# Layer 0's mixer: gate and value columns first, convolution taps spread between later columns, sample taps on GpSimd, weight loads in the queue of the cache copies

## The chip, the cores and the metric

The kernel runs on one core of a Trainium2 chip. The metric is the device time in microseconds (us) of one execution. Before the change three runs gave a median of 2352.38 us (2351.0 to 2361.53).

## What is computed

Two layers of a decoder trunk are evaluated for a prompt of 256 tokens and for 8 samples of 4 tokens each (288 tokens in all, model width 1024, everything in fp32). Only layer 0's mixer is touched. Cut to what matters:

```
z = h @ w_in                                   # 3072 columns and 8 gate columns
glu = z[..., :D_A] * sigmoid(z[..., D_A:o1])   # A: 512 value and 512 gate columns
ca, new_buf_a = causal_dwconv(glu, buf_a, conv_a_w)          # 31 taps per channel
ya = silu(layernorm(ca + conv_a_b, ln_a_g, ln_a_b))
qkv, new_buf_qkv = causal_dwconv(z[..., o1:o2], buf_qkv, conv_qkv_w)   # 1536 columns, 4 taps
q, k = l2norm(silu(q)), l2norm(silu(k))
od, s_new = gated_delta(q, k, v, g, beta, s0)  # chunks of 64 tokens, a triangular solve in each
od = rmsnorm(od, gdn_norm_g) * silu(gate)      # 512 "out" columns
mixed = concat([ya, od]) @ w_out
```

The program must also return the caches of layer 1: for each sample all cached rows but the oldest are copied from an input in HBM to an output in HBM. Those copies depend on nothing and are issued from the start of layer 0's mixer on.

## The kernel before

Channels lie on the 128 partitions and tokens along the free axis. The projection is made in 24 **columns** of 128 channels. A column is 8 accumulating matmuls of 128x128 weights against the 288 tokens, and goes into bank 6 or 7 of PSUM in turn (`acc_of`); so column j may only start when column j-2 has been read out. Weights come in six loads of 2 MB, each holding four columns, into the two slots of `wring` (slot 0 for even loads, slot 1 for odd ones); loads 0 and 1 are issued before the mixer begins.

Each engine runs its own program, and semaphores join them. `col_ready` counts columns that TensorE has finished; `z_ready`, `sig_done`, `glu_done` and `gate_done` count columns that were read out.

The first part of the mixer is written out by hand. It makes the 12 q/k/v columns. ScalarE copies each to SBUF (`take`), VectorE runs its four taps (`convolve`), ScalarE applies silu and squares (`silu`), and TensorE adds up the squares (`sums`). At its end the roots are spread over the partitions (`widen`), q and k are normalized, and the last rows of q/k/v are turned and stored (`q_tails`, `copy_tail`, counted by `tail_q_out`).

The second part is made of lanes: `tile(0)` and `tile(1)` (128 prompt tokens each) and `tile(2)` (the 32 sample tokens) build and solve the triangular systems; `branch()` does all of A, and `main()` walks the four chunks and finishes. Each lane yields a number, its key, ahead of each step, and the step with the smallest key goes next. This fixes the order in which each engine's instructions are written. Steps of a tile have keys 0, 1, 2, ...; `main` starts at 40. In `branch()` the 12 columns of A (4 gate, 4 value, 4 out) start at key 5.5, and the 4 x 31 taps, each an instruction on the prompt and one on the samples, are spread from key 9 up to the layer norm of A at key 50.5.

SyncE issues the small loads, then the 43 cache copies (`roll(n)` issues the next n) in groups of 4, 16 and 23. Before the last group it waits for `tail_q_out`. Then it issues the stores of the new states; it waits for `main`'s last chunk before `out_delta_p`, and its last instruction in the mixer waits until all 14 of its stores have landed (`stored`):

```
sp.wait_ge(turn[2], len(order[2]))
for b in range(DEC_B):
    sp.dma_start(T["out_delta_s"][0, b].rearrange("h k v -> k h v"), S0[:, b, :, :]
                 ).then_inc(stored, 16)
sp.wait_ge(stored, 16 * (6 + DEC_B))
```

The block ends when all engines have come to its end, and layer 0's tail (the expert lookup, which gathers rows of a table in HBM) begins only then. ScalarE issues loads 2 to 5 of the columns' weights and the two of the output projection, in a queue of its own.

Of the kernel before, what the change touches and what calls it, by code (L numbers as in the profile page):

```python
# [16 lines left out]
ALU = mybir.AluOpType  # L17
# [3 lines left out]
D = 1024  # L21
KC = D // 128
# [200 lines left out]
QC = [4, 5, 6, 7, 0, 1, 2, 3, 8, 9, 10, 11]  # L223


def conv_delta_phase(nc, K, T, wring, w_in, w_out_in, mixT, rolls):
# [18 lines left out]
    job_key = lambda j, half: 5.5 + 1.15 * (2 * j + half)  # L245
    JOBS_A = [(kind, c) for c in range(4) for kind in ("gate", "value")] + [("out", c) for c in range(4)]
    MEAN_KEY = MAIN + 10.5
# [16 lines left out]
    with ExitStack() as ctx:  # L264
# [29 lines left out]
        dec, decT = per_tile("decay", [128, 4, 128]), per_tile("decayT", [128, 4, 128])  # L294
# [3 lines left out]
        inT = P.sb("intraT", [128, 3, 4, 128])  # L298
# [18 lines left out]
        a_ready, sig_done, glu_done, gate_done, ca_ready, ln_ready, ln_root, ya_ready, ya_done = (  # L317
            P.sem(n) for n in ("a_ready", "sig_done", "glu_done", "gate_done", "ca_ready", "ln_ready",
# [30 lines left out]
        with nc.Block() as block:  # L349
            @block.sync  # L350
            def _(sp):
# [41 lines left out]
            def _(pe):  # L393
                mm = nc.tensor.matmul

                def column(i):
                    s = i // 4
                    if i % 4 == 0:
                        pe.wait_ge(w_in[s % 2], 16 * (s // 2 + 1))
                    if i >= 2:  # L400
                        pe.wait_ge(z_ready, i - 1)
                    for k in range(KC):
                        last = mm(acc_of(i), wring[:, s % 2, k, i % 4 * 128:i % 4 * 128 + 128], hT[:, k, :],
                                  start=(k == 0), stop=(k == KC - 1))
# [28 lines left out]
                def tile(t):  # L433
# [66 lines left out]
                    for hd in range(GH):  # L500
                        mm(cols_of(t, 0)[:, hd, :], vs[:, hd, :], inT[0:NS, 2, hd, 0:NS], start=True, stop=True)
# [12 lines left out]
                def branch():  # L514

                    for j, (kind, c) in enumerate(JOBS_A):
                        s = {"gate": 3, "value": 4, "out": 5}[kind]
                        for half in range(2):
                            yield job_key(j, half)
                            if half == 0:  # L520
                                pe.wait_ge(w_in[s % 2], 16 * (s // 2 + 1))
                                if j == 0:
                                    pe.wait_ge(z_ready, 11)
# [1986 lines left out]
```

## Time and profile before

| | |
|---|---|
| median of 3 runs | 2352.38 us |
| profiled execution, its own time | 2358.02 us |
| its span | 2356.2 us |
| layer 0's mixer in it | 21.0 to 323.0 us |
| busy share of the span: TensorE / VectorE / ScalarE / GpSimd | 84% / 55% / 32% / 28% |
| mean rate of all transfers | 371 GB/s |

Times in rows are microseconds from the start of the span. In a timeline row the first number is the start, the second the length; "x16" says how many instructions were merged. An engine's name with a q (SPq) is its queue of DMA issues: such a row says when transfers were handed over, not when they landed. A matmul in fp32 appears as two rows' worth of instructions, so a column is x16. "PEclk" is the granted clock of TensorE as a share of 2.4 GHz.

### The profile page before, as it was taken

How to read it: one execution, taken by the hardware profiler on the slowest of the kernel's cores; microseconds unless marked ns; L12 is line 12 of the kernel's file. 1: busy time of each engine (PE TensorE's matmuls, PEld its weight loads, DVE VectorE, ACT ScalarE, POOL GpSimd, SP SyncE). 2: the span in 40 equal slices, each digit the busy share in tenths (PEclk: the TensorE clock that was granted, in tenths of full speed). 3: DMA queues.
4: the chain of work that ended last, by engine and by line, in shares of the span. 5: the costliest groups of instructions: out<-in, count | busy, mean ns of one | idle time of the engine just before them, and what ended most of it. 6: DMA issues, size and time to landing. Idle time of an engine off the chain costs nothing. (4 is left out here: it accounts for less than half of the span.)

```text
span 2356.2 us, 25516 instructions
## 1 busy us (share of the span) xinstructions
PE 1977.2 (84%) x8902; PEld 966.3 (41%) x8902; DVE 1298.6 (55%) x3308; ACT 757.8 (32%) x2225; POOL 653.9 (28%) x650
## 2 busy tenths in 40 slices
PE   7799779887788888866999999989887788888765
PEld 5578645442233332222435654555443233332221
DVE  4485948666667766654100311038666667766754
ACT  3200014343334434433111221124343344434443
POOL 0000004443344354331010000104443444444441
PEclk9897789998999999977999999999999999999977
DMA  9999959999999999997997787828999999999995
GB/s 316 370 333 352 363 194 362 427 426 428 427 427 427 423 405 427 427 427 283 384 392 266 275 308 303 311 112 337 427 427 427 426 427 427 426 427 427 427 427 228
DMA packets 123903, 874.97 MB, mean 371 GB/s; under 512 B 19742, under 2 KB 29726, under 8 KB 38775
## 3 DMA queue, kind: packets, MB, share of 16 engines
q0 software_dynamic: 92160, 662.74, 67.5%
q1 hardware_dynamic: 30751, 198.03, 23.0%
q10 hardware_dynamic: 864, 12.58, 1.4%
q8 instruction: 70, 1.15, 0.2%
q14 instruction: 58, 0.48, 0.1%
HBM read 861.99 MB, written 118.81 MB: 416 GB/s over the span
## 5 line engine op out<-in xcount | busy, mean ns | idle before, releaser
L1570 PE MATMUL tail_acc<-tail_ring,tail_diag 128*128 128x512 f32 x1248 | 617.5, 623 | 131.8 <-ACT tail_diag L1417 130.7
L1717 POOL DMA_INDIRECT tail_ring<-in_peer_uv,tail_idx x348 | 364.9, 1049 | 862.3 <-PE tail_acc L1570 452.6
L1296 DVE CUSTOM_DVE_ANT_0 tail_ring<-tail_ring,all_h 128x1024 f32<-128x1024 f32 x348 | 424.2, 1223 | 261.2 <-DMA tail_ring<-in_peer_uv,tail_idx 259.1
L1570 PE MATMUL tail_acc<-mid_wring,tail_diag 128*128 128x512 f32 x800 | 391.7, 621 | 70.9 <-ACT tail_diag L1417 70.7
L1570 PEld LDWEIGHTS tail_acc<-tail_ring,tail_diag 128*128 128x128 f32 x1248 | 221.4, 193 | 504.0 <-ACT tail_diag L1417 323.2
L1296 DVE CUSTOM_DVE_ANT_0 mid_wring<-mid_wring,all_h 128x1024 f32<-128x1024 f32 x228 | 278.6, 1224 | 172.3 <-DMA mid_wring<-in_peer_uv,tail_idx 172.0
L1409 ACT ACTIVATE tail_gelus<-tail_dots 128x1 f32<-128x1 f32 x576 | 116.4, 202 | 722.5 <-DVE tail_dots L1296 722.1
L1717 POOL DMA_INDIRECT mid_wring<-in_peer_uv,tail_idx x228 | 251.0, 1101 | 319.6 <-PE tail_acc L1570 267.1
L1838 PE MATMUL mix_acc<-mid_wring,all_hT 128*128 128x512 f32 x576 | 273.8, 611 | 1.5 <-PEq L80 1.4
L1570 PEld LDWEIGHTS tail_acc<-mid_wring,tail_diag 128*128 128x128 f32 x800 | 143.8, 194 | 301.8 <-ACT tail_diag L1417 181.5
L1417 ACT ACTIVATE tail_diag<-all_ident,tail_weights 128x128 f32<-128x128 f32 x512 | 205.5, 401 | 24.3 <-PE tail_acc L1570 7.8
L1414 ACT ACTIVATE tail_weights<-tail_gelus,tail_gate 128x1 f32<-128x1 f32 x576 | 169.8, 295 | 18.7
L1838 PEld LDWEIGHTS mix_acc<-mid_wring,all_hT 128*128 128x128 f32 x576 | 103.4, 194 | 110.9 <-issue 110.3
L2062 DVE TENSOR_TENSOR mix_r<-mix_acc,mix_rope 128x128 f32<-128x128 f32 x24 | 7.0, 292 | 188.5 <-ACT mix_rows L2172 188.5
L2089 DVE SCALAR_TENSOR_TENSOR mix_s<-mix_scores_p,mix_band 128x384 f32<-128x384 f32 (+1 forms) x12 | 9.1, 755 | 124.5 <-PE mix_scores_p L1953 124.4
L2379 POOL DMA_DIRECT2D mix_ring<-in_kT x32 | 17.0, 532 | 213.5 <-PE mix_wide L1879 177.7
L1530 PEld LDWEIGHTS tail_spare<-all_hT,tail_w_big 128*128 128x128 f32 x512 | 67.0, 191 | 14.9 <-issue 14.6
L1530 PE MATMUL tail_spare<-all_hT,tail_w_big 128*128 128x128 f32 (+1 forms) x512 | 68.6, 288 | 2.1 <-ACT all_hT L1382 2.1
L1493 PE MATMUL tail_acc<-mid_wring,all_mixT 128*128 128x512 f32 x128 | 60.9, 635 | 3.9 <-PEq L80 3.9
L533 PE MATMUL mix_banks<-all_hT,mid_wring 128*128 128x288 f32 x192 | 56.5, 452 | 3.5 <-DMA mid_wring<-in_w_ab 3.5
L2379 POOL DMA_DIRECT2D mix_ring<-in_v_rows x32 | 16.9, 528 | 149.0 <-PE mix_wide L1916 130.6
L868 DVE SCALAR_TENSOR_TENSOR all_mixT<-mix_padded_a,mix_taps_a,all_mixT 128x256 f32<-128x256 f32 x120 | 56.6, 472 | 0.8
(399 smaller groups left out, 2017.0 us busy)
## 6 DMA issues: line engine op xcount, KB each, us to landing
mid_wring<-in_w_qkv SPq DMA_DIRECT2D x18, 2048.0 KB, 8.9
mix_ring<-in_kT POOLq DMA_DIRECT2D x16, 1024.0 KB, 9.6
mix_ring<-in_v_rows POOLq DMA_DIRECT2D x16, 1024.0 KB, 9.7
out_kv_s<-in_cache_kv_w SPq DMA_DIRECT2D x8, 2016.0 KB, 69.1
mix_ring<-in_kT POOLq DMA_DIRECT2D x16, 768.0 KB, 11.2
mix_ring<-in_v_rows POOLq DMA_DIRECT2D x16, 768.0 KB, 8.6
mid_wring<-in_w_ab ACTq DMA_DIRECT2D x4, 2048.0 KB, 27.2
tail_w_big<-in_w_query SPq DMA_DIRECT2D x8, 1024.0 KB, 11.3
```

Of the source, the lines that this page charges most:

```text
L533: last = mm(acc_of(j), wring[:, s % 2, k, c * 128:c * 128 + 128], hT[:, k, :], start=(k == 0), stop=(k == KC - 1))
L868: ch.step(STT(out=ca[:, c, 0:SEQ], in0=pa[:, c, k:k + SEQ], scalar=wa[:, c, k:k + 1], in1=ca[:, c, 0:SEQ], op0=ALU.mult, op1=ALU.add))
L1296: V.tensor_tensor_reduce(out=u, in0=u, in1=h[:, g, :], scale=1.0, scalar=0.0, op0=ALU.mult, op1=ALU.add, accum_out=dots[:, n:n + 1]).then_ ...
L1409: ch(A(gelus[:, n:n + 1], dots[:, n:n + 1], ACT.Gelu))
L1414: ch(A(weights[:, n:n + 1], gelus[:, n:n + 1], ACT.Copy, scale=gate[:, j, i:i + 1]))
L1417: A(diag[:, n % DIAGS, 0:w], idn[:, 0:w], ACT.Copy, scale=weights[:, n:n + 1]).then_inc(diag_ready, 1)
L1493: last = mm(acc[g][:, c * 512:(c + 1) * 512], mixT[:, k, g * 128:g * 128 + 128], wring[:, c, k, :], start=(k == 0), stop=(k == KC - 1))
L1530: last = mm(sp2[:, i % 2 * 512:i % 2 * 512 + hi - lo], w_query[:, n, k, :], hT[:, k, lo:hi], start=(k == 0), stop=(k == KC - 1))
L1570: last = mm(acc[g][:, c * 512:(c + 1) * 512], diag[:, n % DIAGS, :], v[:, c * 512:(c + 1) * 512], start=first, stop=final)
L1717: pool.indirect_dma_start(slot(r), None, table, bass.IndirectOffsetOnAxis(ap=idx[:, j, i:i + 1], axis=0)).then_inc(landed[r], 16)
L1838: last = mm(acc_of(n), hT[:, kc, o:o + p], w[:, kc, :], start=(kc == 0), stop=(kc == KC - 1))
L2379: pool.dma_start(ring[:, sl % SLOTS_AHEAD, 0:hi - lo], T[name][half, b, :, lo:hi]).then_inc(landed[sl % SLOTS_AHEAD], 16)
```

## The change

The columns come in another order: gate 0, value 0, ..., gate 3, value 3, then the 12 of q/k/v, then the 4 "out" ones. All have one function `column(j)`. Two out columns stand in the written-out part and two in the lanes, at keys 7.5 and 10.5. The taps of A on the prompt are handed out one by one by `tap(n)`: in runs between the gated columns, one after each of the four steps of `convolve` and one at its end, and the last 15 at the start of the lanes. A tap waits for the previous tap of its own channel group only. The taps on the samples leave VectorE: GpSimd multiplies windows of 31 by the taps and adds them up in a tree. `sums` of a q/k column stands three columns later on TensorE. The layer norm of A moves from key 50.5 to 20.5. `decay`, `decayT` and `intraT` of the sample tile become 32 wide. All weight loads move from ScalarE's queue into SyncE's, and the copies are issued between them.

```diff
+AB_COLUMNS = [4, 0, 5, 1, 6, 2, 7, 3] + [8 + n for n in QC] + [20, 21, 22, 23]
-    job_key = lambda j, half: 5.5 + 1.15 * (2 * j + half)
-    MEAN_KEY = MAIN + 10.5
+    OUT_KEYS = {22: 7.5, 23: 10.5}
+    TAILS_KEY = 13.5
+    MEAN_KEY = 20.5
...
-                roll(4)
-                sp.dma_start(S0[:].rearrange("p b h n -> p (b h n)"), T["state_rows"]).then_inc(state_in, 16)
+                for s in range(2, 6):
+                    sp.wait_ge(col_ready, 4 * (s - 1))
+                    sp.dma_start(wring[:, s % 2], T["w_ab"][:, s]).then_inc(w_in[s % 2], 16)
+                    if s == 2:
+                        sp.dma_start(S0[:].rearrange("p b h n -> p (b h n)"), T["state_rows"]).then_inc(state_in, 16)
+                        roll(2)
+                    else:
+                        roll(3)
                 sp.dma_start(T["out_conv_a_s"][0, :, 0:26, :], T["state_conv_a"][0, :, 4:30, :]).then_inc(stored, 16)
-                roll(16)
+                for half in range(2):
+                    sp.wait_ge(col_ready, 20 + 4 * half)
+                    sp.dma_start(wring[:, half], T["w_out0"][:, half]).then_inc(w_out_in[half], 16)
+                    roll(2)
                 sp.wait_ge(tail_q_out, 3)
...
+                for j in range(8, 11):
+                    column(j)
+                for j in range(11, 20):
+                    column(j)
+                    if j < 19:
+                        sums(j - 11)
+                column(20)
                 q_tails(0)
                 q_tails(1)
                 for i in range(8):
                     widen(i)
                 q_tails(2)
+                column(21)
                 lanes.run()
...
-                def load(s):
-                    nc.scalar.dma_start(wring[:, s % 2], T["w_ab"][:, s]).then_inc(w_in[s % 2], 16)
...
+                pool.wait_ge(a_in, 32)
+                for c in range(4):
...
+                    pool.wait_ge(glu_done, c + 1)
+                    ch(G.tensor_tensor(windows[:], shifted, taps_of, ALU.mult))
+                    terms = windows[:].rearrange("p b t k -> p (b t) k")
+                    ch(G.tensor_tensor(terms[:, :, 0:15], terms[:, :, 0:15], terms[:, :, 16:31], ALU.add))
+                    for n in (8, 4, 2):
+                        ch(G.tensor_tensor(terms[:, :, 0:n], terms[:, :, 0:n], terms[:, :, n:2 * n], ALU.add))
+                    ch(G.tensor_tensor(dst, terms[:, :, 0], terms[:, :, 1], ALU.add))
+                    G.tensor_scalar(dst, dst, wa[:, c, 31:32], None, ALU.add).then_inc(samples_done, 1)
...
+                begin_at = (0, 19, 31, 36)
+                taps = sorted(((c, k) for c in range(4) for k in range(CAW)), key=lambda e: (begin_at[e[0]] + e[1], e[0]))
```

**SyncE's queue in the mixer before.** After the small loads come 4 copies (`out_kv_s<-in_cache_kv_w`; 16x15872 is 1.02 MB, 32x16384 is 2.10 MB), the sample states and the other copies:

```order
L371 DMA mix_sample_a<-in_hist_a 128x32x30
L358 DMA out_kv_s<-in_cache_kv_w 16x15872 x4
L374 DMA mix_S_sample<-in_state_rows 128x4096
L375 DMA out_conv_a_s<-in_state_conv_a 8x13312
L358 DMA out_kv_s<-in_cache_kv_w 16x15872 x4
```

After these stand 12 more copies, the two stores behind `tail_q_out`, the other 23 copies, and the stores of the end:

```order
L379 DMA out_conv_qkv_s<-all_h 24x1536
L358 DMA out_kv_s<-in_cache_kv_w 32x16384
L358 DMA out_kv_s<-in_cache_kv_w 32x16128
L358 DMA out_kv_s<-in_cache_kv_w 32x16384
L358 DMA out_kv_s<-in_cache_kv_w 32x16128
L358 DMA out_kv_s<-in_cache_kv_w 32x16384 x19
L382 DMA out_conv_a_p<-all_h 30x512
```

**The same queue of the change.** L382 and L391 are the weight loads, each behind a wait for columns (for 4, 8, 12 and 16 at L382, for 20 and 24 at L391):

```order
L378 DMA mix_sample_a<-in_hist_a 128x32x30
L382 DMA mid_wring<-in_w_ab 128x4096
L384 DMA mix_S_sample<-in_state_rows 128x4096
L365 DMA out_kv_s<-in_cache_kv_w 16x15872 x2
L382 DMA mid_wring<-in_w_ab 128x4096
L365 DMA out_kv_s<-in_cache_kv_w 16x15872 x3
L382 DMA mid_wring<-in_w_ab 128x4096
L365 DMA out_kv_s<-in_cache_kv_w 16x15872 x3
L382 DMA mid_wring<-in_w_ab 128x4096
```

```order
L391 DMA mid_wring<-in_w_out 128x4096
L365 DMA out_kv_s<-in_cache_kv_w 32x16128
L365 DMA out_kv_s<-in_cache_kv_w 32x16384
L391 DMA mid_wring<-in_w_out 128x4096
L365 DMA out_kv_s<-in_cache_kv_w 32x16128
L365 DMA out_kv_s<-in_cache_kv_w 32x16384
L394 DMA out_conv_qkv_p<-all_h 3x1536
```

Between them stand 3 copies of 2 MB and the first `out_conv_a_s`. So 13 copies stand ahead of the second L391 and 30 behind it; the stores of the end (`out_delta_p`, `out_delta_s` x8) stand behind all of them, as before.

**VectorE in a q/k/v column before**, where prompt and sample steps (L753, L756) alternate:

```order
L750 TENSOR_SCALAR mix_conv<-mix_padded_q,mix_taps_q 128x256
L751 TENSOR_SCALAR mix_conv<-mix_sample_q,mix_taps_q 128x32
L753 SCALAR_TENSOR_TENSOR mix_conv<-mix_padded_q,mix_taps_q,mix_conv 128x256
L756 SCALAR_TENSOR_TENSOR mix_conv<-mix_sample_q,mix_taps_q,mix_conv 128x32
L753 SCALAR_TENSOR_TENSOR mix_conv<-mix_padded_q,mix_taps_q,mix_conv 128x256
```

**And of the change**, with a tap of A (L759, into `all_mixT`) behind each pair:

```order
L784 TENSOR_SCALAR mix_conv<-mix_sample_q,mix_taps_q 128x32
L759 SCALAR_TENSOR_TENSOR all_mixT<-mix_padded_a,mix_taps_a,all_mixT 128x256
L788 SCALAR_TENSOR_TENSOR mix_conv<-mix_padded_q,mix_taps_q,mix_conv 128x256
L792 SCALAR_TENSOR_TENSOR mix_conv<-mix_sample_q,mix_taps_q,mix_conv 128x32
L759 SCALAR_TENSOR_TENSOR all_mixT<-mix_padded_a,mix_taps_a,all_mixT 128x256
```

Five taps of A go with each q/k/v column.

**TensorE at the first level of the solve, before** (L461 is the last step of "rows", L467 the step "P 0" of the tiles, L533 columns of A, whole ones at x8 and a half at x4):

```order
L461 MATMUL mix_banks<-all_ident,mix_conv 32x128
L533 MATMUL mix_banks<-all_hT,mid_wring 128x288 x8
L467 MATMUL mix_banks<-mix_decayT,mix_g_wide 128x128 x8
L467 MATMUL mix_banks<-mix_decayT,mix_g_wide 32x32 x4
L533 MATMUL mix_banks<-all_hT,mid_wring 128x288 x4
L473 MATMUL mix_banks<-mix_decay,mix_padded_q 128x128
```

**And of the change**, where the first L420 is column 22 and the second column 23, the last of all 24 (L478 is "rows", L484 is "P 0"):

```order
L478 MATMUL mix_banks<-all_ident,mix_conv 32x128
L420 MATMUL mix_banks<-all_hT,mid_wring 128x288 x8
L484 MATMUL mix_banks<-mix_decayT,mix_g_wide 128x128 x8
L484 MATMUL mix_banks<-mix_decayT,mix_g_wide 32x32 x4
L420 MATMUL mix_banks<-all_hT,mid_wring 128x288 x8
L490 MATMUL mix_banks<-mix_decay,mix_padded_q 128x128
```

The wait for 24 columns in SyncE's queue is a wait for that second L420, which itself stands behind "P 0" of all three tiles.

## Rows read from the trace of the kernel before

**Rows 1.** Part 2 of the page, rate of all transfers in 40 slices.

```profile
GB/s 316 370 333 352 363 194 362 427 426 428 427 427 427 423 405 427 427 427 283 384 392 266 275 308 303 311 112 337 427 427 427 426 427 427 426 427 427 427 427 228
```

**Rows 2.** Timeline of SyncE's queue: cache copies and last stores.

```profile
26.68 5.57 SPq L358 DMA_DIRECT2D out_kv_s<-in_cache_kv_w  x4
...
33.66 10.99 SPq L358 DMA_DIRECT2D out_kv_s<-in_cache_kv_w  x16
...
109.33 38.22 SPq L358 DMA_DIRECT2D out_kv_s<-in_cache_kv_w  x23
...
305.72 6.43 SPq L388 DMA_DIRECT2D out_delta_s<-mix_S_sample  x8
```

**Rows 3.** Windows with copies alone; last three: granted clock, DMA share, GB/s.

```profile
125.00:150.00 25.00, 20.23 (x128) 17.07 (x127) 22.97 (x75) 0.41 (x1) 0.00 (x0) 0.80 1.00 335
150.00:175.00 25.00, 24.69 (x171) 20.82 (x171) 21.00 (x61) 0.41 (x1) 0.00 (x0) 1.00 0.99 326
```

**Rows 4.** The same view, three windows around the mixer's end.

```profile
300.00:303.00 3.00, 2.22 (x9) 1.53 (x9) 1.36 (x3) 0.00 (x0) 0.00 (x0) 1.00 0.60 232
303.00:306.00 3.00, 1.91 (x16) 1.77 (x16) 2.21 (x7) 1.73 (x2) 0.00 (x0) 1.00 0.08 29
...
303.00:360.00 57.00, 42.95 (x198) 23.05 (x199) 28.24 (x85) 9.54 (x18) 2.05 (x2) 0.85 0.46 161
```

**Rows 5.** DMA issues: count, KB each, median us from issue to landing.

```profile
out_kv_s<-in_cache_kv_w SPq DMA_DIRECT2D x8, 2016.0 KB, 69.1
...
out_kv_s<-in_cache_kv_w SPq DMA_DIRECT2D x8, 992.0 KB, 18.5
...
mix_S_sample<-in_state_rows SPq DMA_DIRECT2D x1, 2048.0 KB, 20.4
...
out_kv_s<-in_cache_kv_w SPq DMA_DIRECT2D x40, 77.8
```

**Rows 6.** Waits of SyncE's queue: waited for, us in total, times, longest.

```profile
SPq L349 <- DMA out_delta_s<-mix_S_sample: 2.8, 1, 2.8
```

**Rows 7.** Timeline, TensorE: columns (L403, L533) and the steps around them.

```profile
21.03 11.00 PE L403 MATMUL mix_banks<-all_hT,mid_wring 128*128 128x288 f32 x32 [1.68 <-PEq L80]
...
36.03 8.03 PE L403 MATMUL mix_banks<-all_hT,mid_wring 128*128 128x288 f32 x32
...
48.98 2.95 PE L445 MATMUL mix_banks<-mix_masks,mix_g_wide 128*128 128x128 f32 x24
...
80.80 4.15 PE L403 MATMUL mix_banks<-all_hT,mid_wring 128*128 128x288 f32 x16
...
98.87 8.08 PE L422 MATMUL mix_banks<-mix_roots,all_ident 8*128 8x288 f32 x16 [4.11 <-DVE mix_roots L982]
...
108.70 0.77 PE L453 MATMUL mix_banks<-mix_conv 128*128 128x128 f32 x2 [0.77 <-ACT all_h L654]
...
134.76 4.21 PE L533 MATMUL mix_banks<-all_hT,mid_wring 128*128 128x288 f32 x8
...
259.02 1.06 PE L562 MATMUL mix_banks<-mix_S,mix_Rk 128*64 128x128 f32 x8 [1.06 <-DVE mix_Rk L820]
```

**Rows 8.** Timeline, VectorE: taps of A, a chunk step, roots, the last step.

```profile
96.48 1.94 DVE L980 RECIPROCAL mix_roots<-mix_roots 8x288 f32<-8x288 f32 x1
...
135.36 0.48 DVE L868 SCALAR_TENSOR_TENSOR all_mixT<-mix_padded_a,mix_taps_a,all_mixT 128x256 f32<-128x256 f32 x1
135.75 0.25 DVE L871 SCALAR_TENSOR_TENSOR all_mixT<-mix_sample_a,mix_taps_a,all_mixT 128x32 f32<-128x32 f32 x1
135.92 0.48 DVE L868 SCALAR_TENSOR_TENSOR all_mixT<-mix_padded_a,mix_taps_a,all_mixT 128x256 f32<-128x256 f32 x1
...
309.48 1.36 DVE L937 TENSOR_TENSOR mix_padded_q<-mix_oT 128x1152 f32<-128x1152 f32 x1 [0.22 <-DVE all_mixT L912]
...
321.66 1.35 DVE L950 TENSOR_TENSOR all_mixT<-mix_oT,mix_banks 128x1152 f32<-128x1152 f32 x1 [4.29 <-PE mix_banks L587]
```

**Rows 9.** Groups of GpSimd: a copy of 288 elements per partition.

```profile
L726 POOL COPY mix_sample_q<-mix_hist_q 128x288 f32<-128x288 f32 x1 | 0.5, 474 | 4.3 <-DMA mix_taps_q<-in_taps_q 4.3
```

More of the change, by code:

```diff
@@ L244, in conv_delta_phase @@
     EXPS, MAIN = at[0, "exps act"], 40
-    job_key = lambda j, half: 5.5 + 1.15 * (2 * j + half)
-    JOBS_A = [(kind, c) for c in range(4) for kind in ("gate", "value")] + [("out", c) for c in range(4)]
-    MEAN_KEY = MAIN + 10.5
+    JOBS_A = [(kind, c) for c in range(4) for kind in ("gate", "value")]
+    JOBS_A += [("qkv", i) for i in range(12)] + [("out", c) for c in range(4)]
+    FIRST_QKV, FIRST_OUT = 8, 20
+    OUT_KEYS = {22: 7.5, 23: 10.5}
+    TAILS_KEY = 13.5
+    MEAN_KEY = 20.5
     class Lanes:
@@ L514, in branch @@
                 def branch():
[L516 to L523, printed above, removed]
-                                elif j == 1:
-                                    pe.wait_ge(z_ready, 12)
-                                elif j == 8 or kind == "gate":
-                                    pe.wait_ge(sig_done, j // 2)
-                                elif j == 9 or kind == "value":
-                                    pe.wait_ge(glu_done, (j - 1) // 2)
-                                else:
-                                    pe.wait_ge(gate_done, j - 9)
-                            for k in range(4 * half, 4 * half + 4):
-                                last = mm(acc_of(j), wring[:, s % 2, k, c * 128:c * 128 + 128], hT[:, k, :],
-                                          start=(k == 0), stop=(k == KC - 1))
-                        last.then_inc(a_ready, 1)
-                    yield job_key(12, 0)
+                    for j, key in OUT_KEYS.items():
+                        yield key
+                        column(j)
+                    yield TAILS_KEY
                     pe.wait_ge(last_a_ready, 2)
@@ L884, in branch @@
-                    c = 0
-                    for i in range(len(taps)):
-                        while c < 4 and tap_key(i) > job_key(2 * c + 1, 1) + 0.2:
-                            yield job_key(2 * c + 1, 1) + 0.2
-                            glu(c)
-                            c += 1
-                        yield tap_key(i)
-                        tap(i)
+                    key = at[0, "cross pe"]
+                    yield key
+                    while taps:
+                        tap(4)
+                        key += 0.5
+                        yield key
@@ L968, in _ @@
                     op1=ALU.mult).then_inc(turn["gates"], 1)
-                convolve(2)
+                tap(10)
+                glu(2)
+                tap(6)
                 lanes = Lanes([tile(0), tile(1), tile(2), branch(), main()])
                 lanes.run(at[0, "wide pe"])
-                convolve(3)
+                tap(8)
+                glu(3)
                 lanes.run(at[0, "cross pe"])
-                for i in range(4, 11):
+                for i in range(11):
                     convolve(i)
```

212 lines of the change are left out of this document (104 added, 108 removed).

## Prediction

> **What bounds the kernel now.** I read the page's rates first, to see where transfers are the limit. From slice 8 to 14 layer 0's tail runs at 423 to 428 GB/s, without a dip [rows 1]: there the gathers set the time, so the change can only move the tail's start. The five slices of the mixer move 316 to 363 GB/s [rows 1], which looks like slack. The windows say otherwise: from 125 to 175 us nothing but cache copies moves, the transfer engines are busy 1.00 and 0.99 of the time, and that gives 335 and 326 GB/s [rows 3]. A copy from HBM to HBM is simply slower. So the mixer has two bounds side by side. One is its computing: it goes from 21.0 to the last product at 323.0 [rows 7, 8]. The other is 43 copies of 81.3 MB in all (8 of 1.02, 8 of 2.06 and 27 of 2.10 MB) [rows 5].
>
> SyncE's timeline shows how the second is met: copies start at 26.7, 20 are handed over by 45 and the rest from 109 on [rows 2]. The queue never runs dry, and copies wait in it for 69 and 78 us in the median [rows 5]. They end at about 302: the share is still 0.60 until 303 and then 0.08 [rows 4]. The last stores are issued from 305.7 to 312.2, into an empty queue, and SyncE waits 2.8 us for them [rows 2, 6]; that is 315, 8 us before the computing ends. So today computing sets the mixer's end, with copies 21 us ahead of it. Any change to when copies are issued eats from that margin first.
>
> **The queue.** What stands in SyncE's queue goes in order as far as this trace shows: the sample states were issued at 32.3 behind four copies of 1.02 MB, and landed 20.4 us later, at 52.7 [rows 2, 5]. Four copies from 27 on at 328 GB/s end at 39.4, and 2.1 MB more fill the time to about 46, with the small loads ahead of them not counted; had they shared the engines with the 16 copies issued next, 30 MB, they would have taken far longer. The Trainium skill says the same of where a transfer starts (DMA: Bandwidth & Descriptors, section "Queues, rings and completion order": each engine takes a queue's descriptors in ring order), and warns that completions may still pass each other. By that warning a store could land somewhat before the copies ahead of it, and this trace has no store behind copies that would tell.
>
> **When the 24th column ends.** The new queue holds 30 copies behind the wait for column 23. I therefore lay out TensorE's path to it, from rows of the same steps:
> - Columns 0 and 1 end at 32.0, columns 2 and 3 at 44.1, as before (21.03 + 11.00; 36.03 + 8.03) [rows 7]. Value columns need VectorE to have multiplied the previous pair; it has 19 taps and the gate steps until then. A tap costs 0.395 us from start to start when the next one is independent (135.36 to 135.75), and about 0.52 when it waits for the one ahead, as group 0's first 19 do (0.48 and a handover) [rows 8]. VectorE arrives for value 1 at about 43.8: just in time.
> - Columns 4 to 7 at 4.15 [rows 7], and 1.4 for the gates' sums: 62.2. The wide matmuls, 3.1 [rows 7], and columns 8 to 11: 82.0.
> - Columns 12 to 19, each with one sum of 0.65: 4.8 a column, 120.4. VectorE has per column 2.1 of its own plus five taps, 2.0: 4.1, which is less, so the taps are hidden. So is GpSimd's part, due only when all q/k/v columns are out.
> - Column 20 ends at 124.6. The last convolution ends at 125.2 and then silu, out 0, a table load, root, reciprocal (1.94 [rows 8]) and scaling follow one another: widening starts at about 130.4, takes 8.1 [rows 7], and with the last turned rows (1.0) and column 21 (4.15) TensorE is at 143.6.
> - From the cross products to behind "P 0" of the sample tile took 134.76 - 108.70 = 26.1, nearly all VectorE's [rows 7]; 7 leftover taps add 3: 172.7.
> - Column 23 itself: 4.15, or 8.4 where TensorE has idled (the half column at 134.76 took 4.21 [rows 7]). I take 8.4 here and 2 for the same effect on column 21: 183.
> - GpSimd beside VectorE. GpSimd's 288-element copy took 474 ns, 1.65 ns an element [rows 9]. Its seven steps for one channel group touch 1984 elements: 3.3 us at that price, twice that if a second input doubles it, and some 0.9 of fixed cost; for the three groups ahead of value 3 it is 12 to 22 us. No row shows both engines computing at once. The bounds are 0 (no hindrance) and 22 (full exclusion while VectorE is the pacemaker). I take 5, since the trace's VectorE rows show no slowing anywhere: 188.
>
> The Trainium skill speaks against so small a term (SBUF — State Buffer, section "Who interferes with whom": a VectorE instruction with two SBUF inputs and a GpSimd one that reads SBUF exclude each other for a whole instruction). By that rule the sum would be up to 17 us more; it has its own rival below.
>
> **The copies after that.** Ahead of the wait stand 8 x 1.02 + 5 x 2.08 = 18.6 MB, done by about 145; between, the engines are dry. From 188: the second half of the output weights, 2.1 MB at 427 GB/s [rows 1], 4.9 us; then 30 copies, 62.7 MB at 328 GB/s (between the two windows [rows 3]), 191; then the stores, which before took from 306 to 315 [rows 2, 6], 9. The mixer's last wait ends at 188 + 4.9 + 191 + 9 = 393, against 323: **70 us later**. The ends: 176.5 for the column (no slow columns, no hindrance) gives 58, and 205 gives 87; 326 instead of 335 GB/s is 5 us.
>
> **What computing would do alone.** From behind "P 0" to the first chunk took 259.0 - 134.8 = 124.2 [rows 7]. Of that 10.5 columns of A go, at 4.2 to 8.4 each; at 4.7, 49 us. The layer norm of A comes in, about 7: the first chunk at 172.7 + 124.2 - 49 + 7 = 255, plus 9 for slow columns and hindrance, 264. Four chunks without taps between: 4.5 to 7 us each, 28 with copies; and from the squares to the end 323.0 - 309.5 = 13.5 [rows 8]. Computing would end at about 305, some 18 us earlier than today. Nothing waits for it: the copies cover it by 88 us. Nor does the tail give anything back. The engines were idle 54% of the 57 us from 303 to 360, 31 us [rows 4], and that start-up comes again, only later.
>
> The profiled execution took 2358.0; plus 70 is 2428. The median of the runs is 5.6 lower: **2422 us**.
>
> **Rivals.**
> - Computing sets the end (the faster side). It needs the copies and stores done by 305: with column 23 at 188 that is 62.7 MB in 103 us, 609 GB/s, against 428 as the highest slice [rows 1]. Or column 23 done by 100. For it speaks only that the old queue kept its margin. Time: 2352 - 18 = 2334. Chance 3%.
> - The margin just holds and nothing changes within 0.5%: column 23 would have to end by 130. 3%.
> - The stores pass the copies. Then the mixer ends at 305 with (305 - 193) x 0.328 = 36.7 MB copied and 26 MB left, 79 us of work; 31 of it fits into the tail's idle start [rows 4], 48 pushes the gathers: 48 - 18 = 30 later, 2382. Against it speaks the order shown above. 7%.
> - GpSimd and VectorE exclude each other through the gated columns: 17 us on top, 2439. Against: VectorE idles little there, but part of the delay falls into waits for columns. 15%.
> - The forecast as laid out, 2422, with its bounds 2410 to 2434: 72%.
>
> **How the numbers follow.** The range takes in the forecast's bounds, most of the GpSimd rival and a copy rate up to 340 GB/s: 2400 to 2442. Half a per cent, 12 us, is about what a measurement here can tell from no change. Slower by more: 72 + 15 + 7 = 94%; within: 3%; faster: 3%.
>
> **What would show it.** SyncE's queue waits some 40 us for TensorE's column before the second output weights, at 150 to 190; the transfer share there falls to nothing. Copies end near 385, and SyncE's wait for `out_delta_s` grows from 2.8 us to many tens, while TensorE, VectorE and ScalarE all wait at the block's end from about 305. The q/k/v columns come 4.8 us apart, and no VectorE tap stands in the chunks. The prediction is wrong if copies alone move faster than 345 GB/s, if stores land while copies are queued, or if column 23 ends before 160.

## The result and the profile after

The changed kernel takes 2420.22 us in the median of four executions, the kernel before 2355.85 in the same series (2351.0 to 2361.53). One of the four, at 3271, ran at a granted clock of 0.55 instead of 0.92; the ratio, 1.027 with a 95% interval of 1.023 to 1.031, goes by the other three (2416.24 to 2422.45, median 2417.98). By these the change costs 62 us, where +70 and 2422 had been forecast. The profiled execution has a span of 2420.7 and its own time 2422.45, against 2356.2 and 2358.02.

Where do they lie? The tail's first load is issued at 386.8 instead of 324.3, which is 62.5 later; from there to the end of the span it is 2034 us, and was 2032. The whole loss is in layer 0's mixer.

The rates of the page, as [rows 1], dip to 150 in the third slice (121 to 182 us), where 333 stood:

```profile
GB/s 231 274 150 344 329 329 221 407 427 427 428 427 426 427 413 427 426 427 419 290 361 285 332 221 387 272 146 284 425 426 428 427 427 427 426 427 427 427 426 229
```

SyncE's queue, to hold against [rows 2] (L382 and L391 are weight loads, L365 copies, L401 and L404 stores, L1676 the tail's first load):

```profile
122.87 0.34 SPq L391 DMA_DIRECT2D mid_wring<-in_w_out  x1
123.26 1.18 SPq L365 DMA_DIRECT2D out_kv_s<-in_cache_kv_w  x2
179.86 0.33 SPq L391 DMA_DIRECT2D mid_wring<-in_w_out  x1
180.23 1.14 SPq L365 DMA_DIRECT2D out_kv_s<-in_cache_kv_w  x2
...
182.28 45.24 SPq L365 DMA_DIRECT2D out_kv_s<-in_cache_kv_w  x28
...
294.24 0.41 SPq L401 DMA_DIRECT2D out_delta_p<-mix_S  x1
294.70 87.09 SPq L404 DMA_DIRECT2D out_delta_s<-mix_S_sample  x8
386.77 0.35 SPq L1676 DMA_DIRECT2D tail_gain_a<-in_norm_ffn  x1
```

From 124.4 to 179.9 nothing is issued, and the second load of output weights opens the way for 30 copies. The windows show what the transfer engines do meanwhile (last three columns: granted clock of TensorE, share of the transfer engines, GB/s); with [rows 3] they were at 1.00 and 0.99 in that stretch:

```profile
120.00:140.00 20.00, 15.42 (x52) 9.92 (x50) 13.29 (x33) 5.06 (x12) 0.71 (x2) 0.75 0.99 360
140.00:160.00 20.00, 16.04 (x96) 13.14 (x96) 15.23 (x42) 2.28 (x3) 0.00 (x0) 0.76 0.22 81
160.00:180.00 20.00, 13.84 (x59) 10.62 (x58) 14.46 (x49) 0.55 (x2) 0.00 (x0) 0.73 0.00 0
180.00:200.00 20.00, 19.43 (x183) 17.48 (x182) 13.12 (x26) 2.15 (x3) 0.00 (x0) 1.00 1.01 374
300.00:350.00 50.00, 4.70 (x10) 2.29 (x8) 3.74 (x3) 0.44 (x1) 0.00 (x0) 0.53 1.01 332
350.00:380.00 30.00, 0.00 (x0) 0.00 (x0) 0.00 (x0) 0.00 (x0) 0.00 (x0) 0.50 0.96 315
```

From 309 on the computing engines do nothing; the last two rows hold copies, at 332 and 315 GB/s, and only in their last 4 us stores. Where the copies end is seen in the packets. From 373 to 376 us and from 376 to 379:

```profile
DMA packets 15, 0.98 MB, mean 328 GB/s; under 512 B 0, under 2 KB 0, under 8 KB 0
...
DMA packets 1282, 0.72 MB, mean 239 GB/s; under 512 B 69, under 2 KB 1220, under 8 KB 1282
```

Fifteen packets of 65 KB, then 1282 of some 560 bytes: copies until 376, then the stores of the states, until 385. The waits of SyncE's queue in the mixer (waited for, us in total, times, longest), beside [rows 6]:

```profile
SPq L391 <- PE mix_banks L420: 71.1, 2, 55.4
...
SPq L401 <- DVE mix_S L932: 54.5, 1, 54.5
...
SPq L356 <- DMA out_delta_s<-mix_S_sample: 3.6, 1, 3.6
```

The last row is a trap. The wait for `out_delta_s` is still only 3.6 us. The delay stands in the timeline above: it took 87.09 us to hand over eight stores, where it took 6.43 into the empty queue of before [rows 2]. While what was issued earlier is still under way, the handing over itself stalls, and the trace shows no wait for it.

Computing itself, beside [rows 7, 8]: the last two columns, and the mixer's last instruction:

```profile
159.02 4.82 PE L420 MATMUL mix_banks<-all_hT,mid_wring 128*128 128x288 f32 x16
...
173.79 6.04 PE L420 MATMUL mix_banks<-all_hT,mid_wring 128*128 128x288 f32 x16
```

```profile
307.73 1.35 DVE L955 TENSOR_TENSOR all_mixT<-mix_oT,mix_banks 128x1152 f32<-128x1152 f32 x1 [4.09 <-PE mix_banks L587]
```

Column 23 ends at 179.8, computing at 309.1, which is 14 us earlier than before and 76 us ahead of the mixer's end (385.4: the last store is handed over at 381.8, and SyncE waits 3.6).

### The profile page after: what moved, and what is told of

It is laid out like the page before. It is cut to its first block and busy times, and to the rows that moved or that the text cites. A ratio compares the mean times of both kernels' runs of the same rounds, so it can differ in the third digit from the quotient of the medians.

```text
span 2420.7 us, 25414 instructions
## 1 busy us (share of the span) xinstructions
PE 1983.1 (82%) x8902; PEld 964.8 (40%) x8902; DVE 1291.1 (53%) x3184; ACT 756.3 (31%) x2224; POOL 679.3 (28%) x678
## 5 line engine op out<-in xcount | busy, mean ns | idle before, releaser
L1504 PE MATMUL tail_acc<-mid_wring,all_mixT 128*128 128x512 f32 x128 | 60.8, 634 | 80.4 <-PEq L80 80.4
L420 PE MATMUL mix_banks<-all_hT,mid_wring 128*128 128x288 f32 x384 | 107.1, 440 | 2.0 <-PEq L80 1.7
L420 PEld LDWEIGHTS mix_banks<-all_hT,mid_wring 128*128 128x128 f32 x384 | 78.2, 207 | 29.0 <-issue 5.9
L1504 PEld LDWEIGHTS tail_acc<-mid_wring,all_mixT 128*128 128x128 f32 x128 | 25.6, 204 | 112.1 <-issue 111.8
```

Source lines behind the costliest of these rows:

```text
L420: last = mm(acc_of(j), wring[:, s % 2, k, j % 4 * 128:j % 4 * 128 + 128], hT[:, k, :], start=(k == 0), stop=(k == KC - 1))
L1504: last = mm(acc[g][:, c * 512:(c + 1) * 512], mixT[:, k, g * 128:g * 128 + 128], wring[:, c, k, :], start=(k == 0), stop=(k == KC - 1))
```

## Experiments

Twelve kernels. "Tail at" is the time at which the tail's first load is issued, and "rest" what follows it in the span, both of the profiled execution; the changed kernel stands first, for comparison. The rest lies between 2025 and 2034 us wherever nothing was moved into it or only 3 copies were.

| | ratio to before (95%) | median us | tail at | rest |
|---|---|---|---|---|
| changed kernel | 1.027 (1.023 to 1.031) | 2418.0 | 386.8 | 2034 |
| wait moved behind the copies | 1.0105 (1.0084 to 1.0125) | 2380.4 | 350.7 | 2027 |
| before, new queue alone | 1.0526 (1.0506 to 1.0546) | 2481.0 | 451.2 | 2028 |
| weights in ScalarE's queue | 1.0011 (0.9997 to 1.0026) | 2359.0 | 324.6 | 2030 |
| changed, no copies | 0.9937 (0.9916 to 0.9958) | 2342.0 | 310.1 | 2032 |
| before, no copies | 0.9978 (0.9965 to 0.9991) | 2350.5 | 321.3 | 2034 |
| stores in ScalarE's queue | 1.0235 (1.0216 to 1.0253) | 2413.1 | 385.1 | 2027 |
| queue kept fed | 0.9999 (0.9984 to 1.0015) | 2356.9 | 326.2 | 2031 |
| fed, 3 copies in the tail | 0.9924 (0.9906 to 0.9942) | 2339.5 | 306.9 | 2028 |
| fed, 5 copies in the tail | 0.9988 (0.997 to 1.0006) | 2354.3 | 308.6 | 2042 |
| the same, in small packets | 1.0712 (1.0689 to 1.0734) | 2526.4 | 308.7 | 2217 |
| changed, sample taps later | 1.0244 (1.0215 to 1.0273) | 2414.1 | 383.8 | 2030 |
| fed, 3 copies, sample taps later | 0.9928 (0.9902 to 0.9954) | 2338.9 | 307.6 | 2025 |

**One wait moved.** Only the second load of output weights goes behind the copies:

```diff
-                for half in range(2):
-                    sp.wait_ge(col_ready, 20 + 4 * half)
-                    sp.dma_start(wring[:, half], T["w_out0"][:, half]).then_inc(w_out_in[half], 16)
-                    roll(2)
+                sp.wait_ge(col_ready, 20)
+                sp.dma_start(wring[:, 0], T["w_out0"][:, 0]).then_inc(w_out_in[0], 16)
+                roll(4)
...
                 roll(len(late))
+                sp.wait_ge(col_ready, 24)
+                sp.dma_start(wring[:, 1], T["w_out0"][:, 1]).then_inc(w_out_in[1], 16)
```

> The changed kernel, with one edit in SyncE's queue: the second half of the output weights, with its wait for 24 columns, stands behind all copies and not ahead of 28 of them. Theory (the dry queue is the loss): in the trace of the changed kernel the transfer engines stand nearly idle from about 144 to 180 us; with the wait behind the copies they are fed from 123 on, so the copies end 36 us earlier, at about 348, and the time falls from 2420 to about 2384 (2380 to 2390). Still slower than before, since the first 120 us also left the engines partly idle. Rival (the copies are slowed by something else in the new order, such as GpSimd's or VectorE's work): below 5 us of gain, about 2417.

The tail comes 36.1 us earlier. The idle time of the transfer engines from 140 to 180, by the shares 0.22 and 0.00, had been 35.6. In this kernel the same stretch reads:

```profile
140.00:180.00 40.00, 29.96 (x161) 24.23 (x160) 28.10 (x89) 2.50 (x4) 0.00 (x0) 0.76 1.00 332
```

The columns moved little: column 23 ends at 178.2 instead of 179.8. So idle transfer time before the end is paid one to one, and the rival is out. The kernel is still 25 us slower than before; where that lies, the kernel that keeps the queue fed shows below.

**The new queue on the old kernel.** The weight loads and copies as in the change, each load behind the wait that its slot needs in the old order of columns (the second half behind the twelfth column of A):

```diff
-                roll(4)
-                sp.dma_start(S0[:].rearrange("p b h n -> p (b h n)"), T["state_rows"]).then_inc(state_in, 16)
+                for s in range(2, 6):
+                    if s < 5:
+                        sp.wait_ge(col_ready, 4 * (s - 1))
+                    else:
+                        sp.wait_ge(a_ready, 7)
+                    sp.dma_start(wring[:, s % 2], T["w_ab"][:, s]).then_inc(w_in[s % 2], 16)
...
+                for half in range(2):
+                    sp.wait_ge(a_ready, 8 + 4 * half)
```

> The kernel before with only the queue part of the change: weight loads in SyncE's queue, copies between them in the same numbers, the waits for the columns that free each slot (the second half of the output weights for the last out column, which ends at about 250). Theory (30 copies behind the wait for the last column decide): from that load to the mixer's end it is 206 us, as from 179.9 to 386 in the changed kernel, so the mixer ends near 456 instead of 323, 2488 (2475 to 2498). Rival (the loss belongs to the new order of columns or GpSimd): below 2400.

```profile
247.44 0.33 SPq L387 DMA_DIRECT2D mid_wring<-in_w_out  x1
...
451.18 0.35 SPq L1667 DMA_DIRECT2D tail_gain_a<-in_norm_ffn  x1
```

From the second load to the tail it is 203.7 us here and 206.9 in the changed kernel, with the load at 247.4 and at 179.9. The rule "end = last column + 30 copies + stores" holds over 68 us of difference. It also says what the new order of columns is worth inside the change: without it the new queue costs 124 us instead of 62.

**The queue part undone.** Copies 4, 16 and 23 as before, weights by ScalarE, the rest as changed:

```diff
+                def load(s):
+                    act.wait_ge(col_ready, 4 * (s - 1))
+                    nc.scalar.dma_start(wring[:, s % 2], T["w_ab"][:, s]).then_inc(w_in[s % 2], 16)
...
+                load(2)
                 sigmoid(2)
                 sigmoid(3)
+                load(3)
```

> The changed kernel, with the queue part of the change undone: all weight loads in ScalarE's queue, the copies in groups of 4, 16 and 23 as before. Theory: copies end at 303 to 310 again, but a weight load beside full copies takes 27 us to land (its median before) where it took 7 in the copies' queue, and the new column order gives it only 16 to 20 us; each of the four loads makes TensorE wait 5 to 8 us, about 28 in all, computing ends near 337 instead of 309, and the time is about 2366 (2355 to 2375). Rival (the place of the copies is all that matters, weight loads are hidden): computing ends near 309, stores at about 315, 2344.

```profile
93.29 6.59 PE L411 MATMUL mix_banks<-all_hT,mid_wring 128*128 128x288 f32 x16 [8.06 <-DMA mid_wring<-in_w_ab]
...
115.31 4.15 PE L411 MATMUL mix_banks<-all_hT,mid_wring 128*128 128x288 f32 x16 [0.87 <-DMA mid_wring<-in_w_ab]
...
142.29 5.99 PE L411 MATMUL mix_banks<-all_hT,mid_wring 128*128 128x288 f32 x16 [8.85 <-DMA mid_wring<-in_w_ab]
```

The bracket is the idle time before the row, and what ended it. TensorE waits 17.8 us for weights, where 28 had been expected: the first of the four loads comes in time. Computing ends at 323.3, as before (323.0). A load in a queue of its own took 27.8 us to land in the median, in the copies' queue 7.2. In the changed kernel that queue is often empty, but in the one that keeps it fed (below) the loads landed in 8.2. So the change had a reason to move the loads; the queue's gain is real, and the copies behind the waits are its price.

**No copies.** Both kernels with `rolls = []`, so the 43 copied parts of the output are missing.

> The changed kernel without the 43 cache copies of the mixer (these parts of the output stay unwritten). It shows what the new order of computing takes alone. Theory: the mixer ends at 309 or a few us earlier instead of 386, the time is 2342 (2336 to 2346). The rival, that the end is held by something other than the copies, gives little gain.

> The kernel before without the same 43 copies (these parts of the output stay unwritten). Theory: computing set its end, so little changes: 2350 (2345 to 2356), and the difference to the changed kernel without copies is the 14 us by which the new computing ended earlier (323 against 309). Rival: the weight loads beside the copies had held columns up, then this one gains 10 us or more and the new order of computing is worth little by itself.

```profile
307.48 1.35 DVE L955 TENSOR_TENSOR all_mixT<-mix_oT,mix_banks 128x1152 f32<-128x1152 f32 x1 [4.20 <-PE mix_banks L587]
```

```profile
318.64 1.35 DVE L950 TENSOR_TENSOR all_mixT<-mix_oT,mix_banks 128x1152 f32<-128x1152 f32 x1 [4.29 <-PE mix_banks L587]
```

The first row is of the changed kernel, the second of the one before. Computing ends at 308.8 and 320.0: the new order is worth 11 us in the traces and 8.5 in the medians, a little less than the 14 expected, since the old kernel itself gains 3 us without copies: with them TensorE waits 3.45 us for the last load ahead of the half column at 216.5, without them that half column starts at 213.2 and no wait stands before it. Beside copies the new computing ends 0.3 later.

**Stores in a queue of their own.** All stores of the changed kernel but the first go to ScalarE, which waits for them; SyncE waits only for that first one:

```diff
+                    nc.scalar.dma_start(T["out_delta_s"][0, b].rearrange("h k v -> k h v"), S0[:, b, :, :]
+                                        ).then_inc(act_stored, 16)
+                act.wait_ge(act_stored, 16 * (5 + DEC_B))
```

> The changed kernel, with all stores of the mixer but the first in ScalarE's queue, so that they needn't stand behind copies, and nothing at the mixer's end waits for SyncE's queue. It tries the rival of the prediction in which stores pass the copies (2382). Theory: the mixer ends near 312, but the tail's first loads stand in SyncE's queue behind the copies until about 378, so the tail gets under way only then: 2410 (2400 to 2418). Rival: the tail runs beside the copies and the time is near 2382.

The time came out as forecast, but not for the reason given. The tail begins only at 385, since the stores, alone in their queue, do not get through either. First their issue, then the packets of both queues from 300 to 340 us (q1 copies, q10 stores; packets, MB, share):

```profile
294.50 85.40 ACTq L703 DMA_DIRECT2D out_delta_s<-mix_S_sample  x8
```

```profile
q1 hardware_dynamic: 315, 13.57, 101.3%
q10 hardware_dynamic: 315, 0.16, 1.3%
```

315 packets each: one store packet of 512 bytes for one copy packet of 43 KB. From 340 to 375 it is 301 store packets to 256 of the copies, so the turns are only about one for one. From 375 on, when the copies are done, 4127 store packets go in 9 us. My picture of "stores behind copies" was too narrow; beside them they do no better.

**The queue kept fed.** One wait moved, as above, and copies enough between the loads:

```diff
+                roll(4)
                 for s in range(2, 6):
                     sp.wait_ge(col_ready, 4 * (s - 1))
...
+                    roll((3, 3, 2, 2)[s - 2])
```

> The changed kernel with its weight loads still in the copies' queue, but the queue kept fed: 4 copies are issued ahead of the first wait, then 3, 3, 2, 2 behind the four weight loads, the rest behind the first half of the output weights, and the second half with its wait behind all copies. Theory: the columns keep their times of the changed kernel (copies ahead of a load are done by the time it is issued), computing ends at 309 to 311, the queue is dry for under 10 us in all, copies and second half end near 315 and the stores hold the end until about 318 to 322: 2350 (2345 to 2356). Rival (copies in front delay the weight loads, as in the experiment with the loads in ScalarE's queue): TensorE waits for weights again and computing ends at 320 or later, 2358 or more.

A miss by 7 us: 2356.9. The columns are those of the changed kernel or 1 us ahead, and no load is late, so the rival is out. But the shares from 60 to 80 and from 100 to 120 are 0.83, 7 us of idleness, and the bytes leave no room: 81.3 MB at 328 GB/s, 12.6 MB of weights and 2.1 of states at 427, and 9 of stores make 291 us, from 26.9 on 318; with the 7, 325. The tail came at 326.2. This is also the rest of the change's loss: in the kernel with one wait moved the shares in the five stretches of 20 us from 20 to 120 are 0.54, 0.75, 0.66, 0.67 and 0.84, 31 us of idleness against 7 here, and its tail came 24.5 us later. The new computing ends at 307.8 and waits 18 us. With all 43 copies in it the mixer is bound by transfers at about the time that it took before.

**Three copies in the tail.** The last 3 of the 43 are issued behind the tail's first loads:

```diff
                 sp.dma_start(pT[:], T[f"pT{layer}"]).then_inc(ple_in, 16)
+                for to, frm, done_one in few_copies:
+                    sp.dma_start(to, frm).then_inc(done_one, 16)
```

> As the kernel that keeps the queue fed, and the last 3 of the 43 copies (6.3 MB) are issued by SyncE in layer 0's tail, behind its first loads, where the transfer engines stand idle half of the time. Theory: copies, the second half and the stores end near 302, computing sets the mixer's end at about 309, and 19 us of copies fit into the tail's start: 2342 (2337 to 2348). Rival (the tail's gathers lose what the mixer gains): same as the fed kernel, 2350.

```profile
288.38 13.35 SPq L404 DMA_DIRECT2D out_delta_s<-mix_S_sample  x8
306.86 0.36 SPq L1676 DMA_DIRECT2D tail_gain_a<-in_norm_ffn  x1
```

2339.5, 0.76% faster than before and 3.3% faster than the change. Computing ended at 302.2, 5.6 us earlier than in the fed kernel with the same instructions. Their windows from 200 to 300 differ in the granted clock, 0.74 in the fed kernel (first row), 0.81 here:

```profile
200.00:300.00 100.00, 89.11 (x478) 75.21 (x478) 52.04 (x90) 5.20 (x8) 0.00 (x0) 0.74 1.00 335
```

```profile
200.00:300.00 100.00, 86.60 (x492) 72.33 (x491) 54.43 (x92) 5.63 (x8) 0.00 (x0) 0.81 0.99 332
```

Why the clock was granted differently is open. Little of the gain hangs on it: with 5 copies in the tail (below) computing ended at 307.3, and the tail began at 308.6, only 1.7 later than here. Moving 6.3 MB out of the mixer frees 19 us of transfers, and the tail did come 19.4 us earlier than in the fed kernel.

**Five in the tail.** The same with `rolls[-5:]`.

> The same kernel with 5 copies in the tail instead of 3, GpSimd as in the changed kernel. With 3 the last computing ended at 302.2 and the mixer at about 306, so the stores still held the end by 4 us. Theory: the two copies more free the stores, 3 us less in the mixer, but their 13 us reach into the tail's gathers: 2339 (2334 to 2346), no measurable difference to 3 copies. Rival (the tail has room for them): 2335.

Another miss, 2354.3: the tail starts 1.7 us later than with 3 copies, and then takes 14 us more. Packets from 340 to 356 us, with 5 copies and with 3 (q1 copies and loads, q0 the gathers):

```profile
q1 hardware_dynamic: 111, 5.11, 91.8%
q0 software_dynamic: 51, 0.42, 7.4%
```

```profile
q0 software_dynamic: 610, 4.49, 70.1%
q1 hardware_dynamic: 121, 1.03, 15.8%
```

While copies are under way the gathers (first issued at 342.4 and 340.1) hardly move, 51 packets against 610, and TensorE falls idle:

```profile
355.00:360.00 5.00, 0.71 (x8) 0.55 (x8) 0.00 (x0) 1.35 (x2) 0.94 (x1) 0.75 0.68 221
360.00:365.00 5.00, 0.00 (x0) 0.00 (x0) 1.23 (x2) 0.85 (x3) 0.00 (x0) 0.50 1.01 421
```

That is how the tail loses the time, but not proof that the long packets are what costs it. The two copies more are 4.2 MB, 12.8 us of all transfer engines at 328 GB/s, and the rest of the span grew by 14. Their bytes alone, in a stretch without idle transfer engines, come near the whole loss. The next experiment was meant to tell the two apart.

**Small packets.** Rows of 8 KB are taken every second one, so that neighbours can't be merged:

```diff
+                    to, frm = (ap.rearrange("(a two) n -> two a n", two=2) for ap in (to, frm))
```

> As the kernel with 5 copies in the tail (2354), and those 5 are issued with their rows of 8 KB taken in an order in which neighbours are not merged, so that a packet is at most 8 KB instead of some 43 KB. In the kernel with 5 copies, 51 gather packets (0.42 MB) moved from 340 to 356 us beside 111 packets of the copies; with 3 copies it was 610 (4.49 MB). Theory (the transfer engines serve the queues packet by packet in turn, so a long packet starves a queue of short ones): several hundred gather packets move in that stretch and the time falls to about 2341 (2336 to 2348). Rival (it is only the bandwidth, or the order in SyncE's queue, that the two additional copies take): nothing changes, 2354.

172 us slower than with large packets, and no answer to the question, which stays open. The gathers moved 591 packets from 340 to 356, but the edit had changed something else too. The window from 330 to 340, where little but these copies moves:

```profile
330.00:340.00 10.00, 8.06 (x48) 5.85 (x49) 6.57 (x34) 3.12 (x7) 0.00 (x0) 1.00 0.13 56
```

0.13 of 16 engines are two. The outermost dimension was now 2, and the copies ran on two engines, at 56 GB/s, and beside the gathers for some 300 us more, in which the page's rates stay between 212 and 253 GB/s. That each gather waited for its share on those two engines is how I read it; it wasn't measured by itself. What packets of 8 KB on all 16 would do was not tried.

**Sample taps later.** GpSimd does them behind the last q/k/v column. In the changed kernel:

```diff
+                pool.wait_ge(z_ready, 12)
+                G.tensor_copy(last_q[:, :, 0:3], pq[:, :, SEQ:SEQ + 3]).then_inc(last_q_ready, 1)
...
                 for c in range(4):
                     own = sa[:, c, :, :]
```

> The changed kernel, with GpSimd's sample taps moved behind the last q/k/v column instead of behind each value column. It prices the work of GpSimd beside VectorE. Theory (the two exclude each other; in the changed kernel a channel group's step of 2.1 us holds up a tap of VectorE that takes 0.4 alone): columns 6 and 7 end at 62 to 63 instead of 66.5, and the q/k/v columns keep these 4 us; but GpSimd's 26 us then lie from about 119 to 147, where VectorE paces TensorE, and hinder there instead, so the last column ends within 4 us of 179.8 and the time is 2420 (2413 to 2428). Rival (no exclusion, the 4 us come from something else): columns 6 and 7 still end at 66.5.

VectorE's first taps in the changed kernel and the first one after value 1 (47.49), beside GpSimd's steps; then GpSimd's own; then the same taps of this experiment (the one after value 1 at 44.79):

```profile
33.18 2.26 DVE L755 TENSOR_SCALAR all_mixT<-mix_padded_a,mix_taps_a 128x256 f32<-128x256 f32 x1 [0.23 <-DVE mix_sample_a L768]
35.48 3.97 DVE L759 SCALAR_TENSOR_TENSOR all_mixT<-mix_padded_a,mix_taps_a,all_mixT 128x256 f32<-128x256 f32 x5
...
47.49 2.43 DVE L759 SCALAR_TENSOR_TENSOR all_mixT<-mix_padded_a,mix_taps_a,all_mixT 128x256 f32<-128x256 f32 x1
```

```profile
33.17 2.12 POOL L724 TENSOR_TENSOR mix_windows<-mix_sample_a,mix_taps_a 128x992 f32<-128x992 f32 x1 [7.21 <-DVEq L771]
...
47.49 2.15 POOL L724 TENSOR_TENSOR mix_windows<-mix_sample_a,mix_taps_a 128x992 f32<-128x992 f32 x1 [7.79 <-DVEq L771]
```

```profile
31.73 0.42 DVE L755 TENSOR_SCALAR all_mixT<-mix_padded_a,mix_taps_a 128x256 f32<-128x256 f32 x1 [0.67 <-DMA mix_sample_a<-in_hist_a]
32.18 2.57 DVE L759 SCALAR_TENSOR_TENSOR all_mixT<-mix_padded_a,mix_taps_a,all_mixT 128x256 f32<-128x256 f32 x5
...
44.79 0.48 DVE L759 SCALAR_TENSOR_TENSOR all_mixT<-mix_padded_a,mix_taps_a,all_mixT 128x256 f32<-128x256 f32 x1
...
138.21 5.99 DVE L759 SCALAR_TENSOR_TENSOR all_mixT<-mix_padded_a,mix_taps_a,all_mixT 128x256 f32<-128x256 f32 x8
```

The first tap takes 2.26 us, as long as GpSimd's 2.12 beside it, and 0.42 alone; five more take 3.97 and 2.57. The tap after value 1 takes 2.43 beside a GpSimd step of 2.15, and 0.48 alone. With GpSimd out of the way, columns 6 and 7 end at 60.8 instead of 66.5, and the q/k/v columns 6 us earlier. Then it comes back: the eight taps at 138.21 take 5.99, where they took 3.25 in the changed kernel, and column 23 ends at 179.1 instead of 179.8. The time, 1.0244, can't be told from the changed kernel's 1.027. The hindrance is real, and was only moved.

The same edit on the best kernel:

> The kernel that keeps the queue fed and has 3 copies in the tail, with the sample taps of GpSimd behind the last q/k/v column. Here computing sets the mixer's end. Theory: 4 us gained ahead of column 8 and about as much lost behind the last q/k/v column: 2339 (2334 to 2345). Rival (GpSimd is harmless once the gated columns are done): 2335.

0.9928 against 0.9924: no difference.

## Why the prediction was right

**What bounds the mixer.** Right. With the copies left out of both, the changed kernel is the faster by 0.4%; with them it is slower by 2.7%. The copies, where the new queue puts them, make all of the loss.

**When the 24th column ends.** 188 was forecast, 179.8 measured, inside the bounds of 176.5 to 205. Step by step: columns 4 to 7 ended at 66.5 (62.2 forecast), 8 to 11 at 85.6 (82.0), a q/k/v column takes 4.66 (4.8), column 20 ended at 126.7 (124.6), widening starts at 132.2 (130.4), column 21 ended at 146.3 (143.6) and "P 0" of the sample tile is at 173.2 (172.7). So far the path with no allowance was within 4.3 us, and it had caught up nearly all of them by "P 0". Column 23 took 6.0 and not 8.4, and the 2 for slow matmuls in column 21 were 1.1. The term for GpSimd was put at 5, and about as much came: the lateness at columns 6 and 7 is 4.3, and 5.7 by the experiment. The sum came out late even so, because other terms were too large: columns 8 to 20 took 60.2 and not 62.4, and from column 21's end to "P 0" it was 26.9 and not 29.1. With the 3.3 on columns 21 and 23 that is nearly all of the 8 us. The Trainium skill (SBUF — State Buffer, section "Who interferes with whom") has the mechanism right: the rows above show a VectorE tap with two inputs in SBUF that waits out a whole GpSimd instruction (2.43 us beside 2.15), while the normalizing products, with one input in SBUF and one in PSUM, kept their 0.46 us beside GpSimd (in the run with the later sample taps, from 131 to 138 us). My "no slowing anywhere" in the trace of before said nothing, since the two never compute at the same time there. Its price on the path was 4 to 6 us and not the 17 of the rival: GpSimd computes for some 6.5 us per channel group, of which VectorE lost 3 to 4, and part of that fell into its waits.

**The copies after that.** 4.9 + 191 + 9 forecast; 196.1 from the second load (179.9) to the last copy (376) and 9.4 for the stores. The wait for 30 copies is the mechanism, shown by the two experiments that move the wait.

**What computing would do alone.** 305 forecast, 309.1 measured. The gain over before was put at 18; it is 14 in the traces, and 11 when both run without copies.

**The sum.** The step that was off is column 23 (8 us too late), so 393 for the mixer's end was 385.4. The tail gave back nothing; it took 2 us more, which is within what the rest varies by from run to run. +70 became +64.4 in the profiled executions' own times. That the median, 2422 against 2420.2, came closer still is luck: the base of 2352.4 was the median of three runs, and with a fourth it is 2355.85; and the three executions that the ratio goes by have a median of 2418.0.

Two numbers of the prediction don't follow from its own rows. Column 23 at 205 gives +87, which is 2439, not the 2434 named as the forecast's upper bound, so that bound and the GpSimd rival lie on each other. And the 77.8 us that copies wait in the queue is a median over 40 transfers of which only 27 belong to this mixer; for those 27 it is 100.8. Neither changes the sum.

**The rival of passing stores** failed as argued where the stores stand in the copies' queue: they came only once the copies had ended at 376. It would have failed elsewhere too, for a reason that I had not seen. Moved into another queue they got about one packet of 512 bytes through for each copy packet of 43 KB, and the tail began only 1.7 us earlier.

**What would show it.** The wait ahead of the second output weights (55.4 us), the stretch without transfers, the idle engines from 309, the columns 4.66 apart and chunks without taps (the last one ends at 160.5) all came, and the copies ended at 376 instead of 385. One sign did not come: SyncE's wait for `out_delta_s` stayed at 3.6 us instead of growing to tens, and the time stood in the issue of the stores.

## What to carry to other kernels

Before a wait is put into a queue, count the bytes that are issued behind it: they can't start before it, and where the transfers set the end, as they do here, each idle microsecond comes back there. A load that isn't needed for 100 us has no business ahead of them. Where compute gets faster, ask first whether the transfers had been hidden with room to spare; here there were 21 us of it. With the queue kept fed computing ended 15 us earlier than before and the time was the same; a gain came only with 3 of the copies moved to a stretch with idle transfer engines ahead of the gathers, and it was gone again with 5.

## What the runs showed of the hardware

- Two queues on the same transfer engines take turns by packets, not bytes: 315 and 315 in 40 us, with 0.16 and 13.57 MB, and 301 and 256 in the next 35. The Trainium skill (DMA: Bandwidth & Descriptors, section "Queues, rings and completion order") says that an engine goes round the queues packet by packet, and the trace agrees. Its consequence was new to me: a transfer of short packets gets very little through beside HBM-to-HBM copies, also from another queue (eight stores of 256 KB took 85 us to hand over; gathers, in packets of 8 KB, fell from 610 to 51 in 16 us), while a 2 MB weight load in packets of 15 KB only went from 7.2 to 27.8 us. What that costs the tail beyond the copies' own bytes was not measured.
- The dimension that comes first in a copy's pattern sets how many engines carry it. With 2 there, the share was 0.13 and the rate 56 GB/s. The Trainium skill (DMA: Bandwidth & Descriptors, section "Why a DMA increments its semaphore by 16 and not by 1") states this rule, and the trace agrees; I had not applied it.
- Copies from HBM to HBM alone move at 326 to 335 GB/s, at an engine share of 0.99 to 1.00, where stretches of gathers reach 427 at a share of 1.01.
- A busy queue can hide in the trace. SyncE's long times are rows of issue (45.24 us for 28 copies, 87.09 for eight stores), not waits.
